# A recurrent stage that runs on centred values: mean sums left out, sums and activations moved

## The chip, the core and the metric

One core of a Trainium2 chip runs the whole program. The metric is device time in microseconds (us) of one execution. The engines named here are TensorE (PE, with its weight loads PEld), VectorE (DVE), ScalarE (ACT), GpSimd (POOL) and SyncE (SP, which issues DMAs).

## The reference

Two transformer blocks run one after the other on 512 tokens of width 1024. Of the second, one mixer matters here, an RWKV-7 recurrence with 16 heads of 64:

```python
def step(state, inp):
    r_t, w_t, k_t, v_t, aa_t, bb_t = inp
    sa = jnp.einsum('bhvk,bhk->bhv', state, aa_t)
    state = state * w_t[:, :, None, :] + sa[..., None] * bb_t[:, :, None, :] + v_t[..., None] * k_t[:, :, None, :]
    return state, jnp.einsum('bhvk,bhk->bhv', state, r_t)
...
mean = jnp.mean(y, axis=-1, keepdims=True)
var = jnp.mean(jnp.square(y - mean), axis=-1, keepdims=True)
y = ((y - mean) * lax.rsqrt(var + GN_EPS)).reshape(b, s, c) * lnx_w + lnx_b
bonus = (jnp.sum(r_h * k_h * r_k, axis=-1, keepdims=True) * v_h).reshape(b, s, c)
return ((y + bonus) * g).astype(z.dtype)
```

The mean is taken over the 64 value components of a head. `y` is linear in `v`, and each value component evolves by itself, so the `y` of values whose mean over the components was taken away is `y - mean`. The bonus uses the values as they are.

## The kernel before

Each engine has its own program, written out by hand, and semaphores order them. Weight products are split in three matmuls of 128x512 (high and low halves); one step `n` of `gate_part` is one of them, one step `n` of `rkv_slice` is three.

The recurrent stage goes over 8 pairs of heads (`PAIRS`); a pair fills the 128 partitions and has 8 chunks of 64 tokens. For pair q the stage has these parts, and pairs overlap:

- `wide_part(q)`. PE: `lora_products` (L1257, L1258), 24 steps of `rkv_slice` (L1229 to L1231; steps 0 to 7 make the key, 8 to 15 the receptance, 16 to 23 the value), and between them sums over the partitions of a head, matmuls with a block matrix of ones: `means` (L1279), `bonus_sums` (L1274), `variances` (L1284), `key_norms` (L1267), and the `gate` product (L1290, L1291). `means`, `variances` and `gate` are those of pair q-2, `bonus_sums` that of q-1. DVE: `centred` (L2497), `columns_of`, `log_decays` (L2449 to L2459), `take_key` (L2392, L2394, L2444), `take_bonus` (L2502), the receptance, `finished` (L2508 to L2515), the value. ACT: `sigmoids` (L1867, L1868), `squares_of_centred` (L1884), `decays`, `key_squares` (L1859), `deviations` (L1888), `key_lengths` (L1872).
- `decayed_keys(q)` on DVE (L2465 to L2484) makes the operands of the recurrence, and signals `rk.kr` after L2481.
- `gates(q)` on PE: 48 steps of `gate_part` (L1213), two outputs.
- `prepare(q, step)` on PE and `prepared(q)` on DVE: the 64x64 products of each chunk (L1347) and what takes them; the first, `gram(q, "D")`, waits for `rk.kr`. `turn` turns the values, `bT` and `kkT` by a product with the identity.
- `chain(p)`: the recurrence itself (L1444, L1483), with the steps of `prepare(p+1)` between its links. At its end ACT takes the result of bank 3 out (L1939).

After pair 7 the next stage starts when the last gates have been written to HBM, the residual has been read back (`x_kept`), and POOL has split the first weights of that stage.

POOL does nothing in this stage but split weight strips from `raws` into `whi` (L630) and `wlo` (L632), in two halves each. A strip is split once the products of the strip before it in the same buffer are done. Strip 0 of a pair holds the weights of steps 0 to 15 of `rkv_slice`; strip 2, the gates' weights, takes its place. So step 15 is what lets POOL begin on the gates' strip.

The stage opens with the merge of three attention groups: for four parts `pr`, ACT spreads factors (L1837), PE turns them (L1246), DVE multiplies and adds (L2408 to L2413). Then come ACT's tanh and sigmoids of the low-rank inputs (L1843 to L1845), `lora_products(0)`, 24 gate steps, `key_norms(0)`, 24 more gate steps, `wide_part(1)`, `prepare(0, ...)`.

## Time and profile before

| | |
|---|---|
| time, median of 3 runs | 2182.37 us (2175.4 to 2183.83) |
| time of the profiled execution | 2179.82 us |
| its span | 2178.1 us |
| PE busy / DVE busy / POOL busy / ACT busy | 2079.2 / 1221.7 / 1044.5 / 524.6 us |
| recurrent stage in the span | about 1104 to 1672 us |

In a timeline row the columns are start, duration (both us), engine, line, operation, output and inputs, shapes and count, and in brackets the idle time of the engine before it with what ended that. A time in the span is a position, not a duration.

### The profile page before, as it was taken

The page shows a single profiled execution, that of the slowest core. Times are in us where ns is not written, and L with a number is a line of the kernel's source. Part 1 is how long each engine was busy: PE and PEld are TensorE (multiplying, and loading weights), DVE is VectorE, ACT ScalarE, POOL GpSimd, SP SyncE. Part 2 cuts the span into 40 slices and gives each one's busy share as a digit, 9 for nine tenths or more (in the row PEclk, how much of TensorE's full clock was granted, in tenths as well). Part 3 has the DMA queues.
Part 4 walks back from the last instruction along what each step waited for, and adds up shares of the span by engine and source line. Part 5 has one row for each costly group of instructions (what it writes and reads, how often), then busy time and mean ns, then how long its engine had stood idle before and what let it go on. Part 6 is the DMA issues. An engine that isn't in the chain of part 4 may idle for free.

```text
span 2178.1 us, 39285 instructions
## 1 busy us (share of the span) xinstructions
PE 2079.2 (95%) x16109; PEld 1708.3 (78%) x16109; DVE 1221.7 (56%) x1577; ACT 524.6 (24%) x1132; POOL 1044.5 (48%) x764
## 2 busy tenths in 40 slices
PE   8999999899999989999988999999987999999998
PEld 6888787778777778788867888778875777888887
DVE  7888624466666662301176677776664546656423
ACT  2100002334343121312322212222313013333101
POOL 6777764335344355263453033332203665666663
PEclk9999999899999989999999999999998999999999
DMA  4333232244534331122322122211103332222221
GB/s 139 97 97 97 97 96 69 82 137 130 158 123 133 109 97 59 58 78 70 98 72 61 34 62 61 63 43 34 33 4 128 135 116 78 96 96 96 92 95 65
DMA packets 180341, 189.96 MB, mean 87 GB/s; under 512 B 8141, under 2 KB 161372, under 8 KB 179932
## 3 DMA queue, kind: packets, MB, share of 16 engines
q1 hardware_dynamic: 172288, 181.81, 26.4%
q10 hardware_dynamic: 7900, 5.94, 0.9%
q8 instruction: 116, 1.90, 0.4%
q14 instruction: 37, 0.30, 0.0%
HBM read 179.30 MB, written 8.44 MB: 86 GB/s over the span
## 4 chain that ended last, share of the span: by engine, by line
PE 54%; DVE 10%; DVEq 2%; DMA 2%; ACT 1%; issue 1%; ACTq 0%; POOL 0%; POOLq 0%; SPq 0%
PE bank L775 8%; PE bank L773 8%; PE bank L774 8%; PE bank L1347 6%; PE bank L1444 2%; PE bank L1213 1%; PE bank L1231 1%; PE bank L1229 1%; PE bank L1230 1%; DVE sq L2467 1%; PE bank L1177 1%; PE bank L1149 1%; PE bank L1151 1%; PE bank L1150 1%; PE bank L821 1%; DVE inv_E L2508 1%
## 5 line engine op out<-in xcount | busy, mean ns | idle before, releaser
L632 POOL TENSOR_TENSOR wlo<-raws,whi 128x1024 fp32r<-128x1024 f32 (+5 forms) x316 | 684.9, 2167 | 47.3 <-issue 5.2
L630 POOL TENSOR_SCALAR whi<-raws 128x1024 fp32r<-128x1024 f32 (+5 forms) x316 | 337.9, 1069 | 592.6 <-PE bank L1231 270.4
L773 PE MATMUL bank<-hbuf,whi 128*128 128x512 f32 (+2 forms) x840 | 328.5, 391 | 0.0
L775 PE MATMUL bank<-hbuf,wlo 128*128 128x512 f32 (+2 forms) x840 | 327.6, 390 | 0.0
L774 PE MATMUL bank<-hbuf,whi 128*128 128x512 f32 (+2 forms) x776 | 302.7, 390 | 0.0
L606 POOL TENSOR_TENSOR spare<-ones 1x1 f32<-1x1 f32 x100 | 25.3, 253 | 464.2 <-PE bank L775 252.9
L773 PEld LDWEIGHTS bank<-hbuf,whi 128*128 128x128 f32 (+2 forms) x840 | 157.2, 187 | 34.6 <-POOL wlo L632 1.1
L775 PEld LDWEIGHTS bank<-hbuf,wlo 128*128 128x128 f32 (+2 forms) x840 | 157.1, 187 | 34.4
L774 PEld LDWEIGHTS bank<-hbuf,whi 128*128 128x128 f32 (+2 forms) x776 | 145.1, 187 | 31.4
L2346 DVE TENSOR_REDUCE nmax<-bank 128x4 f32<-128x512 f32 (+3 forms) x40 | 21.1, 550 | 159.9 <-PE bank L1124 116.7
L1229 PE MATMUL bank<-hbuf,whi 128*128 128x512 f32 x192 | 87.9, 458 | 0.0
L1213 PE MATMUL bank<-hbuf,whi 128*128 128x512 f32 x256 | 84.3, 406 | 0.0
L1231 PE MATMUL bank<-hbuf,wlo 128*128 128x512 f32 x192 | 75.7, 394 | 0.0
L1230 PE MATMUL bank<-hbuf,whi 128*128 128x512 f32 x192 | 75.5, 393 | 0.0
L2198 DVE SCALAR_TENSOR_TENSOR adaacc<-adaw,vec,adaacc 128x768 f32<-128x768 f32 x56 | 71.6, 1278 | 5.4 <-DMA adaw<-in_w_ada 0.3
L773 PE MATMUL bank<-fH,whi 128*128 128x512 f32 x176 | 68.7, 390 | 0.0
L775 PE MATMUL bank<-fH,wlo 128*128 128x512 f32 x176 | 68.5, 389 | 0.0
L774 PE MATMUL bank<-fL,whi 128*128 128x512 f32 x176 | 68.5, 389 | 0.0
L908 PE MATMUL bank<-hbuf,whi 128*128 128x512 f32 x160 | 66.7, 417 | 1.1 <-DVE y2L L2183 0.9
L803 PE MATMUL bank<-hbuf,whi 128*128 128x512 f32 x128 | 54.3, 424 | 10.9 <-DVE hbuf L737 5.8
L910 PE MATMUL bank<-hbuf,wlo 128*128 128x512 f32 x160 | 62.8, 393 | 0.0
L652 ACT ACTIVATE sq<-xT 128x512 f32<-128x512 f32 x24 | 15.2, 632 | 185.6 <-DVE xT L2115 144.0
(482 smaller groups left out, 4676.3 us busy)
## 6 DMA issues: line engine op xcount, KB each, us to landing
adaw<-in_w_ada SPq DMA_DIRECT2D x64, 384.0 KB, 4.2
raws<-in_w_up SPq DMA_DIRECT2D x22, 1024.0 KB, 4.9
raws<-in_w_in SPq DMA_DIRECT2D x41, 512.0 KB, 4.3
raws<-in_w_in SPq DMA_DIRECT2D x18, 1024.0 KB, 4.9
raws<-in_pool_w_in SPq DMA_DIRECT2D x16, 1024.0 KB, 5.2
raws<-in_mla_w_in SPq DMA_DIRECT2D x10, 1024.0 KB, 5.9
raws<-in_pool_w_out SPq DMA_DIRECT2D x8, 1024.0 KB, 5.0
raws<-in_mla_w_out SPq DMA_DIRECT2D x8, 1024.0 KB, 5.4
```

Source lines behind the costliest of these rows:

```text
L630: G.tensor_scalar(h_, r_, 1.0, 1.0, ALU.mult, ALU.mult)
L632: G.tensor_tensor(l_, r_, f32(h_), ALU.subtract).then_inc(raw_split, 1)
L773: M.matmul(dst, wh, acts[k][0], start=(first and k == 0), stop=False)
L774: M.matmul(dst, wh, acts[k][1], start=False, stop=False)
L775: mm = M.matmul(dst, wl, acts[k][0], start=False, stop=(last and k == n - 1))
L908: M.matmul(dst, wh, act[0], start=first, stop=False)
L1213: mm = M.matmul(dst[:, :], wl if i == 2 else wh, h_out[k][int(i == 1)], start=(k == 0 and i == 0), stop=(k == DT - 1 and i == 2))
L1229: M.matmul(bank[z][:, :], wh, h_out[k][0], start=(k == 0), stop=False)
L1230: M.matmul(bank[z][:, :], wh, h_out[k][1], start=False, stop=False)
L1231: mm = M.matmul(bank[z][:, :], wl, h_out[k][0], start=False, stop=(k == DT - 1))
L1347: mm = M.matmul(dst[rows, cs], left[rows, cs], R, start=(start is None or c == start), stop=True, skip_group_check=True)
L2198: V.scalar_tensor_tensor(adaacc[:, :], adaw[n % 3][:, :], c_col, adaacc[:, :], ALU.mult, ALU.add)\
```

## The change

The values are turned by a product with `centre`, the identity less 1/64, instead of the identity. Everything of the recurrence that is linear in the values is then centred, and `means` (PE), `centred` (DVE) and the wait of `squares_of_centred` (ACT) go; ACT squares straight out of bank 3 at the end of the chain (`gn.q`). `variances` moves forward to just behind the first two steps of `rkv_slice` (in the last wide part, six gate steps). In `wide_part(1)` alone, `bonus_sums(0)` moves from behind step 7 to behind step 15, with a wait for the taken gates in its old place. `key_norms(0)` moves nine gate steps back. ACT's tanh and sigmoids move to behind the first and second spread of the merge. `centre` lies where an unused buffer of the same size was, and two small DVE instructions make it at the start.

```diff
@@ -233,7 +233,7 @@
-        margin = sb("margin", [P, 96])
+        centre = sb("centre", [P, 96])[:, 0:CH]
         raws = sb("raws", [P, 2 * 2048])
@@ -376,7 +376,7 @@
                              "E32": inv_E32, "N2": tile(hf, 0), "W": tile(hf, 0), "A2": tile(hf, 1), "Z": tile(hf, 1)}
-                    gn_y, gn_c, gn_sq, gn_dev = inv_DA, inv_U, inv_E16, inv_E32
+                    gn_x, gn_y, gn_sq, gn_dev = inv_DA, inv_U, inv_E16, inv_E32
         with ExitStack() as st:
@@ -1263,7 +1263,7 @@
                 elif q >= 2:
-                    pe.wait_ge(sem("gn.y"), q - 1)
+                    pe.wait_ge(sem("gn.q"), q - 1)
                 M.matmul(bank[3][:, :], same[64][:, :], tile(sq, 0), start=True, stop=True)\
@@ -1273,11 +1273,6 @@
                     .then_inc(sem("rk.bs"), 1)
-
-            def means(p):
-                pe.wait_ge(sem("gn.y"), p + 1)
-                M.matmul(bank[4][:, :], same[64][:, :], gn_y[:, :], start=True, stop=True)\
-                    .then_inc(sem("gn.m"), 1)
@@ -1298,16 +1293,18 @@
                 lora_products(q)
+                rkv(0, 2)
                 if q >= 2:
-                    means(q - 2)
-                rkv(0, 8)
+                    variances(q - 2)
+                rkv(2, 8)
                 if q >= 2:
                     pe.wait_ge(sem("inv.dve"), q * TAKEN_ALL)
-                bonus_sums(q - 1)
-                rkv(8, 12)
-                if q >= 2:
-                    variances(q - 2)
-                rkv(12, 16)
+                    bonus_sums(q - 1)
+                else:
+                    pe.wait_ge(sem("gt.taken"), 2)
+                rkv(8, 16)
+                if q == 1:
+                    bonus_sums(0)
                 key_norms(q)
@@ -1328,22 +1325,25 @@
-                means(PAIRS - 2)
-                for n in range(9):
+                for n in range(6):
+                    gate_part(PAIRS - 1, n)
+                variances(PAIRS - 2)
+                for n in range(6, 9):
                     gate_part(PAIRS - 1, n)
...
                 bonus_sums(PAIRS - 1)
-                variances(PAIRS - 2)
                 for n in range(9, 3 * DT):
...
+            identity = chunk_mask["id"]
+
             def chunk_products(dst, left, right, lo=0, hi=CHUNKS, start=None):
...
                     for rows in HEAD_ROWS:
-                        R = ident[rows, rows] if right is None else right[rows, cs]
+                        R = right[rows, 0:CH] if right is identity or right is centre else right[rows, cs]
                         mm = M.matmul(dst[rows, cs], left[rows, cs], R, start=(start is None or c == start),
@@ -1365,8 +1365,8 @@
-            def turn(b, x, signal):
-                chunk_products(bank[b], x, None).then_inc(sem(signal), 1)
+            def turn(b, x, signal, by=identity):
+                chunk_products(bank[b], x, by).then_inc(sem(signal), 1)
@@ -1381,7 +1381,8 @@
                     pe.wait_ge(sem("inv.dve"), q * TAKEN_ALL + levels_taken(k))
-                chunk_products(bank[LEVEL_BANK[k][w]], inv_t[left], None if right == "I" else inv_t[right])                    .then_inc(sem(f"inv.pe{w}"), 1)
+                chunk_products(bank[LEVEL_BANK[k][w]], inv_t[left],
+                               identity if right == "I" else inv_t[right]).then_inc(sem(f"inv.pe{w}"), 1)
@@ -1397,7 +1398,7 @@
                     pe.wait_ge(sem("rk.ge"), q * 8 + GRAM_TAKEN["ak"])
-                    turn(7, vT[q % 2], "rk.tv")
+                    turn(7, vT[q % 2], "rk.tv", centre)
                 elif step == 7:
@@ -1492,9 +1493,11 @@
                 gate_part(0, n)
+            pe.wait_ge(evac[0], fill("rkv", 0) + 1)
+            for n in range(3 * DT, 3 * DT + 9):
+                gate_part(0, n)
             key_norms(0)
-            pe.wait_ge(evac[0], fill("rkv", 0) + 1)
-            for n in range(3 * DT, 6 * DT):
+            for n in range(3 * DT + 9, 6 * DT):
                 gate_part(0, n)
@@ -1508,7 +1511,6 @@
                     last_wide_part()
-            means(PAIRS - 1)
             variances(PAIRS - 1)
@@ -1836,13 +1838,15 @@
                            f.unsqueeze(3).to_broadcast([P, 4, 2, 64])).then_inc(sem("cmb.f"), 1)
-
-
-            for b in (0, 2, 3):
-                act.wait_ge(evac[b], fill("lora", b) + 1)
-            A.activation(wlow[0:64, :], wlow[0:64, :], ACT.Tanh).then_inc(sem("lora.act"), 1)
-            A.activation(tile(glow, 0), tile(glow, 0), ACT.Sigmoid)
-            A.activation(glow[0:32, S:2 * S], glow[0:32, S:2 * S], ACT.Sigmoid).then_inc(sem("lora.act"), 1)
+                if pr == 0:
+                    act.wait_ge(evac[0], fill("lora", 0) + 1)
+                    A.activation(wlow[0:64, :], wlow[0:64, :], ACT.Tanh).then_inc(sem("lora.act"), 1)
+                if pr == 1:
+                    for b in (2, 3):
+                        act.wait_ge(evac[b], fill("lora", b) + 1)
+                    A.activation(tile(glow, 0), tile(glow, 0), ACT.Sigmoid)
+                    A.activation(glow[0:32, S:2 * S], glow[0:32, S:2 * S], ACT.Sigmoid).then_inc(sem("lora.act"), 1)
+
@@ -1879,10 +1883,6 @@
-            def squares_of_centred(p):
-                act.wait_ge(sem("gn.c"), p + 1)
-                A.activation(gn_sq[:, :], gn_c[:, :], ACT.Square).then_inc(sem("gn.q"), 1)
-
             def deviations(p):
@@ -1896,8 +1896,6 @@
                         load_lora(q + 1)
-                if q >= 2:
-                    squares_of_centred(q - 2)
                 if more:
@@ -1933,10 +1931,9 @@
                 act.wait_ge(sem("sq.y"), p + 1)
-                if p + 1 < PAIRS:
-                    act.wait_ge(sem("inv.pe0"), (p + 1) * MADE_ALL[0] + level_made(0, 4))
                 act.wait_ge(sem("rk.y"), p + 1)
                 A.activation(gn_y[:, :], bank[3][:, :], ACT.Copy, scale=SCAN_SCALE ** -2).then_inc(sem("gn.y"), 1)
+                A.activation(gn_sq[:, :], bank[3][:, :], ACT.Square, scale=SCAN_SCALE ** -2).then_inc(sem("gn.q"), 1)
@@ -1954,7 +1951,6 @@
             load_gate(PAIRS - 1)
-            squares_of_centred(PAIRS - 1)
             deviations(PAIRS - 1)
@@ -2050,6 +2046,7 @@
                     V.tensor_copy(chunk_mask[name][r, :], x[r, r])
+                V.tensor_scalar(centre[r, :], ident[r, r], 1.0 / CH, None, ALU.subtract)
             V.tensor_reduce(res4[:, :], ident[:, :].rearrange("p (k r) -> p r k", r=4), AX.X, ALU.add)
@@ -2492,22 +2489,17 @@
-            def centred(p):
-                dve.wait_ge(sem("gn.m"), p + 1)
-                V.scalar_tensor_tensor(gn_c[:, :], bank[4][:, :], -1.0 / 64, gn_y[:, :], ALU.mult, ALU.add)\
-                    .then_inc(sem("gn.c"), 1)
-
             def take_bonus(q):
...
-                x, pc = gn_y, pcol[p % 3]
+                x, pc = gn_x, pcol[p % 3]
                 dve.wait_ge(sem("gn.s"), p + 1)
...
                 dve.drain()
-                V.scalar_tensor_tensor(x[:, :], gn_c[:, :], pc[:, 8:9], gn_dev[:, :], ALU.mult, ALU.mult)
+                V.scalar_tensor_tensor(x[:, :], gn_y[:, :], pc[:, 8:9], gn_dev[:, :], ALU.mult, ALU.mult)
                 dve.drain()
@@ -2518,7 +2510,7 @@
                 if q >= 2:
-                    centred(q - 2)
+                    dve.wait_ge(sem("gn.y"), q - 1)
                 if more:
@@ -2606,7 +2598,6 @@
             take_last_gates()
-            centred(PAIRS - 1)
             finished(PAIRS - 1)
...
```

## Rows read from the trace of the kernel before

**Rows 1.** Page, part 1: busy time, share of the span, instructions.
```profile
PE 2079.2 (95%) x16109; PEld 1708.3 (78%) x16109; DVE 1221.7 (56%) x1577; ACT 524.6 (24%) x1132; POOL 1044.5 (48%) x764
```
**Rows 2.** Windows: stretch, its length, busy of each engine, granted clock, DMA.
```profile
1157.00:1162.00 5.00, 5.00 (x11) 3.19 (x11) 1.99 (x6) 3.83 (x4) 0.00 (x0) 0.50 0.05 13
1240.00:1305.00 65.00, 63.48 (x1074) 52.95 (x1072) 45.56 (x59) 16.80 (x39) 18.99 (x12) 1.00 0.18 53
```
**Rows 3.** Timeline of wide part 2 and the chain after it.
```profile
1237.02 0.60 ACT L1939 ACTIVATE inv_DA<-bank 128x512 f32<-128x512 f32 x1 [0.43 <-PE bank L1444]
...
1239.15 1.12 PE L1279 MATMUL bank<-inv_DA,same 128*128 128x512 f32 x2
...
1240.31 0.69 DVE L2497 SCALAR_TENSOR_TENSOR inv_U<-bank,inv_DA 128x512 f32<-128x512 f32 x1 [1.42 <-PE bank L1279]
...
1253.03 0.75 DVE L2392 TENSOR_SCALAR Rr<-bank,pcol 128x512 f32<-128x512 f32 x1 [2.63 <-PE bank L1231]
1253.16 1.05 POOL L630 TENSOR_SCALAR whi<-raws 128x1024 fp32r<-128x1024 f32 x1 [40.05 <-PE bank L1231]
...
1275.83 1.15 PE L1347 MATMUL bank<-aT,bT 64*64 64x64 f32 x32 [0.53 <-DVE rT L2481]
```
**Rows 4.** Chain that ended last, wide part 4: start, length, what.
```profile
1368.37 1.05 PE bank L1279 x2
...
1378.53 0.86 PE bank L1284 x2
```
**Rows 5.** Timeline of ACT in the merge, and at the first decays.
```profile
1110.53 1.14 ACT L1837 COPY ap<-fac 128x512 f32<-128x512 f32 x2 [1.62 <-PE bank L1246]
...
1115.96 1.14 ACT L1837 COPY ap<-fac 128x512 f32<-128x512 f32 x2 [3.77 <-PE bank L1246]
...
1123.60 1.28 ACT L1844 ACT_TABLE_LOAD   x1
...
1145.75 0.63 ACT L1876 ACTIVATE epos<-cc 128x512 f32<-128x512 f32 x1 [1.77 <-DVE lwd L2459]
```
**Rows 6.** Timeline from the first gates to the end of wide part 1.
```profile
1139.66 1.13 PE L1267 MATMUL bank<-sq,same 128*128 128x512 f32 x2 [1.42 <-ACT sq L1859]
...
1156.70 2.08 PE L1274 MATMUL bank<-Rr,same 128*128 128x512 f32 x2 [3.70 <-DVE Rr L2484]
...
1159.96 0.43 DVE L2449 TENSOR_SCALAR lwd<-lwd 128x512 f32<-128x512 f32 x1 [2.69 <-ACT inv L1868]
1160.46 1.23 DVE L2451 TENSOR_TENSOR_SCAN cc<-restart,lwd 128x512 f32<-128x512 f32 x1
...
1162.86 0.69 DVE L2459 TENSOR_TENSOR lwd<-cc,lwd 128x512 f32<-128x512 f32 x1
...
1166.01 1.04 POOL L630 TENSOR_SCALAR whi<-raws 128x1024 fp32r<-128x1024 f32 x1 [15.51 <-PE bank L1231]
1166.34 1.13 PE L1267 MATMUL bank<-sq,same 128*128 128x512 f32 x2 [0.49 <-ACT sq L1859]
...
1172.98 0.75 DVE L2392 TENSOR_SCALAR vT<-bank,pcol 128x512 f32<-128x512 f32 x1 [5.28 <-PE bank L1231]
```
**Rows 7.** Timeline: DVE instructions issued while POOL runs one.
```profile
1129.04 2.35 POOL L632 TENSOR_TENSOR wlo<-raws,whi 128x1024 fp32r<-128x1024 f32 x1
1129.86 2.07 DVE L2411 TENSOR_TENSOR num<-num 128x512 f32<-128x512 f32 x1
...
1262.83 2.41 POOL L632 TENSOR_TENSOR wlo<-raws,whi 128x1024 fp32r<-128x1024 f32 x1
...
1264.19 1.33 DVE L2465 TENSOR_SCALAR sq<-sq 128x512 f32<-128x512 f32 x1
```
**Rows 8.** One line of DVE: count, duration ns min/median/max, first and last start.
```profile
L2510 DVE SCALAR_TENSOR_TENSOR inv_DA<-inv_U,pcol,inv_E x8: 752/2695/2695, 1258.1 to 1663.4; 128x512 f32<-128x512 f32 x8
```
**Rows 9.** Chain that ended last, from the last chain to the next stage.
```profile
1655.99 2.67 DMA gates_kept<-xT
1659.05 9.45 DMA raws<-in_w_att_out
...
1671.60 0.79 PE bank L821
```

## The prediction, made before the result was known

> **What bounds the kernel now.** I read the page first: PE is busy nearly all of the span, and nothing else comes near [rows 1]. Then the chain that ended last, over the recurrent stage. It alternates: PE through the first two thirds of a wide part, then DVE, then PE and DVE link by link. A timeline of one wide part shows the seams [rows 3]. DVE waits 2.63 us for the receptance product (step 15) at 1253.03. From there it works without a pause to `rk.kr`, and PE, which has meanwhile done the gates, waits only 0.53 us for it at 1275.83. So a wide part is set by PE up to step 15, and then by DVE with PE just behind: what PE saves before step 15 moves both, and is gained in full. The clock is 1.00 there [rows 2].
>
> The opening is another matter [rows 6]. PE waits 3.70 us for the first bonus operand at 1156.70, then computes steps 8 to 15 at a granted clock of 0.50, which is 1.2 GHz [rows 2], and is through just before `key_norms(1)`, which waits 0.49 us for the squares. Those come from DVE's list: decays from 1159.96, then the key. Steps 16 to 23 follow at full clock and end with DVE's take of the value at 1172.98, DVE having waited 5.28. So there the order is DVE up to the squares, then PE.
>
> **Means and centring in the wide parts.** `means` is two matmul instructions that take 1.05 on the chain, its sister `variances` 0.86 [rows 4]. The extra 0.19 stands behind `lora_products`, and I take it that whatever comes next pays it. Saving 0.86 for each of seven: wide parts 2 to 7 and the last. That is 6.0 us; at most 7 x 1.05 = 7.4. `variances` is moved, not added. It waits for ACT's new square: the copy ends at 1237.62, a square of the same form takes 0.60 too, so `gn.q` comes at about 1238.2, and PE is at `means` only at 1239.15 [rows 3] and at the new place later still. Behind that wait stand the key steps, untouched. DVE loses its 1.42 wait and the 0.69 of the centring [rows 3], and its decays start some 2 us sooner, but it waits 2.63 at step 15 afterwards, so nothing comes of it beyond PE's 0.86. If that wait were not there, DVE would set the pace and `means` be worth nothing. ACT's square is in its list either way.
>
> **The last pair.** After it PE waits for a chain of DMAs: the last gates are written, then `x_kept` and the weights are read, 9.45 us, and PE begins at 1671.60 [rows 9]. That chain starts at the last gate product, which the change leaves where it is. The norm of pair 7 is ready sooner (1.05 of `means`, 0.69 of centring, some 0.3 between: 2 us), and that is hidden: 0, at most 2.0.
>
> **Tanh and sigmoids in the merge.** ACT has 1.62 us free before the second spread and 3.77 before the third [rows 5]. An activation of this size takes 0.60 [rows 3]: the tanh fits the first gap, a table load of 1.28 and two sigmoids (1.2) fit the second. They do not hold up the spreads, and PE did not wait for them where they were (it waited for DVE's last multiplication). 0 both ways. Without the slack it would cost 0.6 + 1.28 + 1.2 = 3.1.
>
> **`key_norms(0)` nine steps later.** PE waited 1.42 for it [rows 6], and now waits about that longer for the receptance instead, then does nine steps and the norm. It reaches `wide_part(1)` 0.86 later. ACT's lengths and decays come up to 2.6 later against 1.77 of slack [rows 5], and DVE has the whole norming of the keys before it asks for them: 0. PE's 0.86 disappears in the 3.70 wait.
>
> **`bonus_sums(0)` behind step 15.** PE no longer stands still in front of the bonus operand. It had steps 0 to 7 done at 1156.70 - 3.70 = 1153.0; with the 0.86 that is 1153.9. Eight steps at full clock last what they last behind `key_norms(1)`: 1172.98 - 1166.34 less 1.05 for the norm's matmuls, 5.6. So step 15 is done at 1159.5, where it was done just before 1166.01. That gains nothing by itself, for `key_norms(1)` still waits for DVE's and ACT's squares. It does two other things.
>
> First, it lets POOL loose. POOL had waited 15.51 us for step 15 and began at 1166.01 [rows 6]. Now it begins at 1159.6, and its four instructions (1.05, 2.4, 1.05, 2.4) lie on top of DVE's decays. The trace shows what that does [rows 7]: L2411, issued at 1129.86 under a POOL instruction that ends at 1131.39, ends at 1131.93, 0.54 behind it, and takes 2.07; L2465 takes 1.33 and ends 0.28 behind POOL's. DVE instructions on SBUF operands stand until POOL's is over, and get one turn between two of POOL's. Worked through: L2449 ends at 1160.9 (POOL's first is over at 1160.65); POOL's second until 1163.3; the scan L2451 then, until 1164.4; POOL's third until 1165.45, and the small copy; POOL's fourth until 1168.0; L2455 until 1168.5; the rest to 1169.4. The decays ended at 1163.55 [rows 6], so they are 5.9 late. No row shows a scan under a POOL instruction; if it runs through, the same sum gives 1168.4, 4.9 late. I take 5.4. If nothing collided it would be 0.5 or less, from small shifts of the split before it.
>
> The Trainium skill, "SBUF — State Buffer", section "Who interferes with whom", says that GpSimd and VectorE share one pair of ports as an exclusive lock, and that a VectorE instruction with two SBUF inputs is blocked as well. The rows agree for L2411; by that rule the scan is blocked, and the sum below would be 0.5 higher.
>
> Second, PE now idles from about 1160.4 until the squares at about 1171.7, three times as long as in the 3.70 after which it worked at half clock [rows 2, 6]. So the norm and steps 16 to 23 are slow instead of steps 8 to 15, and nothing hides them: a sum and eight steps lasted 1166.01 - 1156.70 = 9.3 after the idle, against 1172.98 - 1166.34 = 6.6 warm. That is 2.7 more; 0 if the clock stays.
>
> **Small things.** Two 64x64 instructions on DVE at the start, each at most the 0.43 of a 128x512 one [rows 6]: 0.2. The turning product has the same shape, 0.
>
> **The sum.** -6.0 + 5.4 + 2.7 + 0.2 = +2.3 on the profiled execution's 2179.8, so 2182.1. The median of the runs is 2.5 above that execution, and the forecast against it is 2182.4 + 2.3 = 2184.7. What a measurement of this kernel can tell from no change is about 0.5%, 10.9 us, so this is no measurable change.
>
> **Rivals.**
> - *The forecast, opening loses what the wide parts gain:* 2184.7, between -7.4 + 4.9 + 2.9 = +0.4 (2182.8) and -6.0 + 5.9 + 2.9 = +2.8 (2185.2), and 3 more to each side for the measurement. Chance 0.47.
> - *POOL does not hurt.* DVE wins the turns or POOL comes too late; the cold clock stays. -6.0 + 0.5 + 2.7 + 0.2 = -2.6, 2179.8. For it: which engine goes first decides, and the rows have only one order. Against it: six DVE instructions on SBUF in a row. Chance 0.20.
> - *The opening costs nothing, and all of `means` and the last pair counts:* -7.4 - 2.0 = -9.4, 2173.0. For it: half clock and lock both depend on small shifts. Against it: 9.45 us of DMA in front of the next stage. Chance 0.17.
> - *The change does not do what it says:* DVE is the bound in the wide parts after all, and the 0.86 is not gained. +8.3, 2190.7. For it: PE's wait at 1275.83 is for DVE. Against it: DVE's own wait of 2.63. Chance 0.08.
> - *Slower.* In the wide parts too the phase of DVE and POOL shifts. L2510 stands behind POOL in most pairs now (2.695 against 0.752) [rows 8]; were one more instruction caught, it costs 1.94 in each of six parts, 11.7: 2184.7 + 11.7 = 2196.4. It decides from 8.6 us more than the forecast, 1.4 a part. Against it: DVE and POOL are both released by step 15, within 0.13 of each other [rows 3], and stay so. Chance 0.08.
>
> **How the numbers follow.** The likeliest case gives 2184.7. A range from 2174 to 2192 leaves out the slower case and half of the fast one, 0.16 to 0.2, and takes in both ends of the collision and of the clock. Faster by over 0.5% needs more than 10.9 us, which no case gives alone; a third of the fast case with luck in the measurement: 0.06. Slower: the last case and some of the one before it, 0.09. The rest, 0.85, is within 0.5%.
>
> **What would show it.** Means: no L1279; from one wide part to the next 0.86 less than now, (1368.37 - 1239.15) / 2 = 64.6 [rows 3, 4]. Opening: POOL L630 released at about 1159.6 instead of 1166.0, L2455 or L2451 two to three times as long as now, `key_norms(1)` with an idle of some 11 us before it, a granted clock of 0.50 behind it, and the value taken at about 1181 instead of 1172.98. End: PE's wait for POOL at the next stage longer by about 2, its start as far behind the last gate product as now. The prediction is wrong if `gn.q` holds PE at `variances`, if the key steps are not what DVE waits for, or if POOL's earlier start brings a transfer forward that delays another.

## The result, and the profile after

The changed kernel took 2185.75 us in the median of 20 runs, and the kernel before 2182.11 in the median of 20 runs on the same chip: +3.6 us. Three of these 40 runs were slow, 2611.53 to 3455.23 us, and are left out of the ratio. It is 1.0021, with a 95% interval from 1.0014 to 1.0028, so 3.1 to 6.1 us. The forecast was 2184.7, +2.3. By the 0.5% that the chances were drawn with, this is no change. The interval excludes 1, so with so many runs a small loss is measurable, and it also excludes the +2.3: the loss is larger than the sum said.

The profiled execution took 2186.43, with a span of 2184.7. Part 1 of its page, which answers to [rows 1]:

```profile
PE 2070.0 (95%) x16093; PEld 1703.5 (78%) x16093; DVE 1217.3 (56%) x1571; ACT 524.2 (24%) x1132; POOL 1045.0 (48%) x764
```

PE has 16 matmul instructions fewer and is 9.2 us less busy, and the span is longer. So PE stands idle somewhere. Three stretches tell where.

**The wide parts.** The timeline of wide part 2 in the kernel after (L1279 is now `variances`, L2389 the take of a product, L2478 the last key step):

```profile
1219.31 1.10 PE L1347 MATMUL bank<-aT,bT 64*64 64x64 f32 x32
...
1248.83 1.02 PE L1279 MATMUL bank<-inv_E,same 128*128 128x512 f32 x2
...
1260.35 0.75 DVE L2389 TENSOR_SCALAR Rr<-bank,pcol 128x512 f32<-128x512 f32 x1 [3.57 <-PE bank L1231]
...
1283.15 1.15 PE L1347 MATMUL bank<-aT,bT 64*64 64x64 f32 x32 [0.54 <-DVE rT L2478]
...
1536.82 1.15 PE L1347 MATMUL bank<-aT,bT 64*64 64x64 f32 x32 [0.53 <-DVE rT L2478]
```

The first and the last of the same products (L1347, the first Gram product of a pair) in the kernel before:

```profile
1211.68 1.10 PE L1347 MATMUL bank<-aT,bT 64*64 64x64 f32 x32
...
1533.39 1.15 PE L1347 MATMUL bank<-aT,bT 64*64 64x64 f32 x32 [0.53 <-DVE rT L2481]
```

There is one norm product where [rows 3] had `means` at 1239.15 and `variances` later, and nothing holds it. DVE's wait for the receptance product grew from 2.63 to 3.57: it is idle longer, so PE still sets the pace there. PE's wait for the key steps is what it was (0.54 against 0.53). From one Gram product to the next the five periods from 1219.31 to 1536.82 are 63.50 in the mean. Before, from 1211.68 to 1533.39, they were 64.34. That is 0.84 less in each. The sixth period, up to the last pair, is 61.09 where it was 61.97.

**The opening.** The timeline from the first key steps to the take of the value, in the kernel after (L2446 to L2456 are the decays):

```profile
1148.02 0.62 POOL L630 TENSOR_SCALAR whi<-raws 128x512 fp32r<-128x512 f32 x1 [12.83 <-PE bank L1213]
...
1148.86 1.76 DVE L2466 TENSOR_TENSOR kk<-kk,sq 128x512 f32<-128x512 f32 x1
1150.70 0.93 DVE L2469 SCALAR_TENSOR_TENSOR aT<-kk,lwd 128x512 f32<-128x512 f32 x1
1151.56 1.77 DVE L2470 TENSOR_TENSOR bT<-kk,inv 128x512 f32<-128x512 f32 x1
...
1160.20 1.04 POOL L630 TENSOR_SCALAR whi<-raws 128x1024 fp32r<-128x1024 f32 x1 [7.41 <-PE bank L1231]
1160.87 0.65 DVE L2446 TENSOR_SCALAR lwd<-lwd 128x512 f32<-128x512 f32 x1 [2.69 <-ACT inv L1872]
1161.39 2.34 POOL L632 TENSOR_TENSOR wlo<-raws,whi 128x1024 fp32r<-128x1024 f32 x1
1161.59 3.21 DVE L2448 TENSOR_TENSOR_SCAN cc<-restart,lwd 128x512 f32<-128x512 f32 x1
1163.69 1.95 POOL L630 TENSOR_SCALAR whi<-raws 128x1024 fp32r<-128x1024 f32 x1
1164.88 0.79 DVE L2450 COPY mid<-cc 128x8 f32<-128x8 f32 x1
...
1165.79 2.84 POOL L632 TENSOR_TENSOR wlo<-raws,whi 128x1024 fp32r<-128x1024 f32 x1
1166.51 2.14 DVE L2455 TENSOR_TENSOR fade<-cc,mid 128x7 f32<-128x7 f32 x1
1168.58 0.68 DVE L2456 TENSOR_TENSOR lwd<-cc,lwd 128x512 f32<-128x512 f32 x1
...
1172.05 2.08 PE L1267 MATMUL bank<-sq,same 128*128 128x512 f32 x2 [11.16 <-ACT sq L1863]
...
1180.20 0.75 DVE L2389 TENSOR_SCALAR vT<-bank,pcol 128x512 f32<-128x512 f32 x1 [6.78 <-PE bank L1231]
```

And the window behind PE's idle time (columns as in [rows 2]; the last two figures are DMA):

```profile
1172.00:1176.00 4.00, 3.95 (x9) 2.50 (x10) 1.34 (x2) 1.88 (x2) 0.00 (x0) 0.60 0.00 0
```

POOL begins at 1160.20 where it began at 1166.01 [rows 6], and DVE's decays interleave with it. The scan takes 3.21 instead of 1.23. The copy of eight elements a row takes 0.79 and the product of seven 2.14, as each waits for a turn. PE does nothing for 11.16 us, and its next product takes 2.08, as one did after the idle of 3.70 [rows 6]. The granted clock behind it is 0.60 in the mean of four us, so a part of them ran at 1.2 GHz; from 1176 on it is 1.00. The value is taken at 1180.20 instead of 1172.98. `lora_products(0)` came 0.84 earlier (1129.03, before at 1129.87). The merge itself is as long as before, the whole stage began 0.81 earlier in this execution. So from `lora_products(0)` to the take of the value the opening costs 7.22 + 0.84 = 8.1. Three parts make it up. The decays begin 1.75 later after `lora_products(0)` (31.84 against 30.09), before POOL touches them. They take 4.80 longer. From `key_norms(1)` to the take there are 8.15 where there were 6.64, 1.51 more.

**The last pair.** Timeline from the last gates to the next stage, kernel after:

```profile
1657.86 0.37 SPq L507 DMA_DIRECT2D gates_kept<-xT  x1
...
1668.60 4.90 DVE L2608 TENSOR_TENSOR rL<-yr,rH 128x512 fp32r<-128x512 f32 x8
1670.26 3.29 POOL L606 TENSOR_TENSOR spare<-ones 1x1 f32<-1x1 f32 x1 [85.66 <-DMA raws<-in_w_att_out]
...
1675.60 0.80 PE L821 MATMUL bank<-atH,whi 128*128 128x512 f32 x1 [14.60 <-POOL wlo L632]
```

From the write of the gates to PE's start there are 17.74 us, where there were 15.61 (1655.99 to 1671.60, [rows 9]). POOL's instruction on a single element, the first that it does when the weights have landed, took 3.29, where it took 0.61 before.

Between `lora_products(0)` and PE's start on the next stage there are 546.57 us, before 541.73: 4.8 more. The spans of the two profiled executions differ by 6.6. The rest lies outside of the stage (0.84 earlier ahead of it, 2.6 later behind it), where the change does next to nothing.

### The profile page after: what moved, and what is told of

Same layout as the page of the kernel before. It is cut to its first block, busy times and chain, and to the rows that moved or that the text cites. A ratio compares the mean times of both kernels' runs of the same rounds, so it can differ in the third digit from the quotient of the medians.

```text
span 2184.7 us, 39249 instructions
## 1 busy us (share of the span) xinstructions
PE 2070.0 (95%) x16093; PEld 1703.5 (78%) x16093; DVE 1217.3 (56%) x1571; ACT 524.2 (24%) x1132; POOL 1045.0 (48%) x764
## 4 chain that ended last, share of the span: by engine, by line
PE 53%; DVE 9%; DMA 2%; DVEq 2%; issue 1%; ACT 1%; POOL 1%; POOLq 0%; ACTq 0%; SPq 0%
PE bank L775 8%; PE bank L774 8%; PE bank L773 8%; PE bank L1347 7%; PE bank L1445 2%; PE bank L1213 1%; PE bank L1229 1%; PE bank L1231 1%; PE bank L1230 1%; DVE sq L2464 1%; PE bank L1177 1%; PE bank L1149 1%; PE bank L1151 1%; PE bank L1150 1%; DVE inv_E L2500 1%
## 5 line engine op out<-in xcount | busy, mean ns | idle before, releaser
L1213 PEld LDWEIGHTS bank<-hbuf,whi 128*128 128x128 f32 x256 | 48.2, 189 | 17.1 <-DVE Rr L2391 4.2
```

The costliest lines, as they stand in the source:

```text
L1213: mm = M.matmul(dst[:, :], wl if i == 2 else wh, h_out[k][int(i == 1)], start=(k == 0 and i == 0), stop=(k == DT - 1 and i == 2))
```

## The experiments

The time beside each is the median of its own runs. The kernel before ran on the same chip with each group of them: 2181.74 (bonus product back, POOL held, POOL held with PE at work, bonus product alone), 2181.31 (both back, with the wait, the wait in the changed kernel) and 2181.35 (the other four). A difference from before is from that of its own group, and two kernels of different groups are compared by these differences; the changed kernel's is +3.6. None of these differences is good to a tenth. The 95% intervals reach 2 to 3 us to each side, and more where two experiments are set against each other. In the text cold stands for a granted clock of 0.50 (1.2 GHz), warm for 1.00 (2.4 GHz).

### `bonus_sums(0)` back in its old place

```
-                    bonus_sums(q - 1)
-                else:
-                    pe.wait_ge(sem("gt.taken"), 2)
-                rkv(8, 16)
-                if q == 1:
-                    bonus_sums(0)
+                bonus_sums(q - 1)
+                rkv(8, 16)
```

> The changed kernel, with bonus_sums(0) back behind step 7 of wide part 1. Theory: its place behind step 15 cost 8.1 us (POOL's split on top of DVE's decays 5.4, half clock behind the long idle 2.7), so this runs 8.1 under the changed kernel, 4.5 under the kernel before (-0.2%). Rival (the opening costs nothing, the loss sits at the end of the stage or is luck): like the changed kernel, 3.6 above the kernel before.

2181.21, 0.5 under the kernel before; ratio 0.9997 (0.9988 to 1.0006). Against the changed kernel that is 3.6 + 0.5 = 4.1 gained. It should have been 4.5 under before, so 4 are missing: something else costs too. In its timeline the second norm product is this:

```profile
1168.75 2.01 PE L1267 MATMUL bank<-sq,same 128*128 128x512 f32 x2 [2.21 <-ACT sq L1859]
```

PE waited 2.21 for the squares, where it had waited 0.49 [rows 6], and it worked at half clock behind so short an idle (granted 1.00 from 1166.50 to 1168.70, 0.53 from there to 1171.00).

### POOL held back, clock left cold

The changed kernel, with POOL made to wait before the first split of the gates' strip until DVE has the key of pair 1:

```
+                        if ph == "rkv" and i == 1 and j == 2:
+                            pool.wait_ge(sem("rk.kk"), 2)
```

> The changed kernel, in which POOL waits with the gates' strip of pair 1 until DVE has made the key of pair 1. Nothing else moves. Theory: the port collision is 5.4 to 5.9 of the loss, so 1.8 to 2.3 under the kernel before; the scan takes 1.23 again instead of 3.21, key_norms(1) idles some 6 us instead of 11.16 and is still followed by half clock (2.08 for its two matmuls). Rival (the clock or the order alone costs it): 3.6 above the kernel before, key_norms(1) as late as in the changed kernel.

2180.43, 1.3 under before; ratio 0.9998 (0.9989 to 1.0007). Against the changed kernel 3.6 + 1.3 = 4.9 gained. Its timeline:

```profile
1141.97 1.02 PE L1269 MATMUL bank<-sq,same 128*128 128x512 f32 x2
...
1160.11 1.23 DVE L2450 TENSOR_TENSOR_SCAN cc<-restart,lwd 128x512 f32<-128x512 f32 x1
...
1165.45 1.04 POOL L632 TENSOR_SCALAR whi<-raws 128x1024 fp32r<-128x1024 f32 x1 [14.53 <-DVE kk L2443]
...
1165.98 2.08 PE L1269 MATMUL bank<-sq,same 128*128 128x512 f32 x2 [6.51 <-ACT sq L1865]
...
1175.51 0.75 DVE L2391 TENSOR_SCALAR vT<-bank,pcol 128x512 f32<-128x512 f32 x1 [8.17 <-PE bank L1233]
```

The scan is back at 1.23, and the norm comes 6.3 us sooner after `lora_products(0)` than in the changed kernel (36.75 against 43.02). Not all of that is POOL's doing: in this execution the clock stayed at full through `key_norms(0)` (1141.97), and the decays already began 1.5 sooner. The other 4.8 are the decays, 3.58 long against 8.39. The cold clock behind `key_norms(1)` stays.

### POOL held back, and PE kept at work

The same, and 24 products without use behind `bonus_sums(0)`:

```
+                    for n in range(24):
+                        M.matmul(bank[4][:, :], h_out[1][0][:, 0:P], h_out[0][0], start=True, stop=True)
```

> As the one before, and PE fills its idle time ahead of key_norms(1) with 24 matmuls of 128x512 into a bank that nobody reads (5.4 us of work, not part of the computation). Theory: the clock stays at full, another 2.7 is gained: 4.5 under the kernel before; the value is taken 6.6 behind the start of key_norms(1) instead of 8.15. Rival (the clock costs nothing): like the one before, or up to 1 us slower.

2177.87, 3.9 under before; ratio 0.9983 (0.9974 to 0.9992). It is 2.6 under the run without these products. Its timeline, with POOL's first instruction for the next stage:

```profile
1165.94 1.13 PE L1269 MATMUL bank<-sq,same 128*128 128x512 f32 x2 [0.88 <-ACT sq L1867]
...
1172.59 0.75 DVE L2393 TENSOR_SCALAR vT<-bank,pcol 128x512 f32<-128x512 f32 x1 [5.28 <-PE bank L1233]
...
1663.62 0.31 POOL L606 TENSOR_TENSOR spare<-ones 1x1 f32<-1x1 f32 x1 [86.45 <-DMA raws<-in_w_att_out]
```

The norm takes 1.13 instead of 2.08, and from its start to the take of the value there are 6.65 instead of 9.53: 2.9 for the clock, where POOL is held back. The 2.6 between the medians is not that price alone. The norm stands 1.5 later after `lora_products(0)` than in the run above, whose first norm ran at full clock. And in this execution POOL's instruction on one element took 0.31 and PE started the next stage 15.19 behind the write of the gates, 17.73 in the run above.

### `bonus_sums(0)` moved, alone, in the kernel before

```
-                bonus_sums(q - 1)
+                    bonus_sums(q - 1)
+                else:
+                    pe.wait_ge(sem("gt.taken"), 2)
...
+                if q == 1:
+                    bonus_sums(0)
```

> The kernel before, with the move of bonus_sums(0) behind step 15 alone. Theory: it costs 8.1 by itself: 2190 where the kernel before takes 2182 (+0.37%). Rival (the loss comes from the parts together): no change.

2189.84, 8.1 above before; ratio 1.0035 (1.0021 to 1.0048), so between 4.6 and 10.5. Its timeline shows both signs with nothing else changed:

```profile
1161.69 3.22 DVE L2455 TENSOR_TENSOR_SCAN cc<-restart,lwd 128x512 f32<-128x512 f32 x1
...
1172.15 2.07 PE L1267 MATMUL bank<-sq,same 128*128 128x512 f32 x2 [11.16 <-ACT sq L1863]
```

One thing differs from the kernel before that the edit doesn't touch. The first norm, `key_norms(0)`, took 2.07 in this execution and 1.13 in the profiled one of before, and the decays began 1.68 later after `lora_products(0)`. So the 8.1 holds a cold first half of the opening too.

### Both products of the opening back

The first edit, and `key_norms(0)` in its old place:

```
+            key_norms(0)
             pe.wait_ge(evac[0], fill("rkv", 0) + 1)
-            for n in range(3 * DT, 3 * DT + 9):
-                gate_part(0, n)
-            key_norms(0)
-            for n in range(3 * DT + 9, 6 * DT):
+            for n in range(3 * DT, 6 * DT):
```

> The changed kernel with bonus_sums(0) and key_norms(0) both back in their old places: centring and the moved activations alone. Theory: seven times 0.86, 6.0 under the kernel before, less what DVE's earlier end costs at the start of the next stage (2.1 in the profiled execution of the changed kernel): 4 to 6 under. Against the kernel with only bonus_sums(0) back, key_norms(0) accounts for 0 to 1. Rival (the wide parts gain nothing): no change.

2177.84, 3.5 under before, where 4 to 6 were expected; ratio 0.9982 (0.997 to 0.9994). It ran again in a later group:

> bonus_sums(0) and key_norms(0) both back, the same program as the earlier one with both back: how well 3.5 us under the kernel before repeats beside the others of this call. 3 to 6 under.

2177.33, 4.0 under; ratio 0.9976 (0.9966 to 0.9986). With the bonus product alone put back it was 0.5 under, so the kernel with `key_norms(0)` nine steps later is 3.0 to 3.5 slower, which the prediction had at 0. What is left are the centring, the earlier `variances` and the merge, and the six us expected of them are not all there: the end is still as in the changed kernel. The timeline of the first of the two runs:

```profile
1660.11 4.90 DVE L2602 TENSOR_TENSOR rL<-yr,rH 128x512 fp32r<-128x512 f32 x8
1661.79 3.26 POOL L606 TENSOR_TENSOR spare<-ones 1x1 f32<-1x1 f32 x1 [85.71 <-DMA raws<-in_w_att_out]
...
1667.10 0.79 PE L821 MATMUL bank<-atH,whi 128*128 128x512 f32 x1 [14.61 <-POOL wlo L632]
```

### The end: DVE waits for POOL's first strip

Before the fifth low half of the next stage, DVE waits until POOL has split the first half strip of that stage's weights:

```
                 dve.wait_ge(sem("mx.hi"), k + 1)
+                if k == 4:
+                    dve.wait_ge(raw_split, split_value(STRIP0["mix"], 0))
```

On top of both products back:

> As the one before, and DVE waits with the low halves of the recurrence's output until POOL has split the first half strip of the next stage. Theory: POOL's one-element instruction no longer stands 3.29 us behind DVE: 2.1 less than the one before, 6 to 8 under the kernel before. Rival (the DMA sets the start anyway, or DVE's later splits hold PE later): no change against the one before.

2175.95, 5.4 under before, where 6 to 8 were expected; ratio 0.9971 (0.9961 to 0.9981). In its timeline POOL's one-element instruction is short again:

```profile
1665.89 0.18 POOL L606 TENSOR_TENSOR spare<-ones 1x1 f32<-1x1 f32 x1 [85.83 <-DMA raws<-in_w_att_out]
```

Once more, in the later group:

> Both back, and DVE waits with the low halves until POOL's first half strip is split, again: 2 under the one without that wait if the port lock at the end is real; the rival says equal.

2176.02, 5.3 under; ratio 0.9966 (0.9954 to 0.9978). The wait gained 1.9 in the one group and 1.3 in the other; each by itself is within the noise. In the traces, from the write of the gates to PE's start on the next stage there are 14.70 us in both of these runs, where the two of "both back" have 17.74 and 17.73. And in the changed kernel as it is:

> The changed kernel with that wait of DVE alone. Theory: 2.1 less than the changed kernel, 1.5 above the kernel before. Rival: like the changed kernel, 3.6 above.

2182.74, 1.4 above before; ratio 1.0005 (0.9995 to 1.0015), where the changed kernel is 3.6 above: 2.2 gained. In its trace the stretch is 16.02, against 17.74.

### `key_norms(0)` moved, alone, in the kernel before

The edit of "both back", the other way round.

> The kernel before, with the move of key_norms(0) behind nine gate steps alone. The kernel with only bonus_sums(0) put back ran 0.5 us under the kernel before where 4.5 was expected, and the one with both put back 3.5 under; the difference is laid to this move: a longer first idle of PE brings half clock, POOL's split of the value strip comes 2.3 later and falls on DVE's key work. Theory now: 2 to 4 us above the kernel before. Rival (the first prediction: the 0.86 disappears in a wait): no change.

2184.74, 3.4 above before by the medians; ratio 1.0008 (0.9999 to 1.0017), so between nothing and 3.7. By itself this does not show a loss. The timeline of this run:

```profile
1140.47 1.22 PE L1213 MATMUL bank<-hbuf,whi 128*128 128x512 f32 x2 [3.75 <-DVE Rr L2396]
...
1149.66 0.62 POOL L630 TENSOR_SCALAR whi<-raws 128x512 fp32r<-128x512 f32 x1 [13.58 <-PE bank L1213]
...
1150.67 1.60 DVE L2471 TENSOR_TENSOR kk<-kk,sq 128x512 f32<-128x512 f32 x1
1152.35 0.93 DVE L2474 SCALAR_TENSOR_TENSOR aT<-kk,lwd 128x512 f32<-128x512 f32 x1
1153.21 1.78 DVE L2475 TENSOR_TENSOR bT<-kk,inv 128x512 f32<-128x512 f32 x1
```

and the kernel before at the same place, rows that the prediction did not look at:

```profile
1146.13 3.35 DVE L2467 RECIPROCAL sq<-sq 128x512 f32<-128x512 f32 x1
1146.42 0.62 POOL L630 TENSOR_SCALAR whi<-raws 128x512 fp32r<-128x512 f32 x1 [10.38 <-PE bank L1213]
...
1149.56 1.49 DVE L2469 TENSOR_TENSOR kk<-kk,sq 128x512 f32<-128x512 f32 x1
1151.13 0.69 DVE L2472 SCALAR_TENSOR_TENSOR aT<-kk,lwd 128x512 f32<-128x512 f32 x1
1151.74 0.68 DVE L2473 TENSOR_TENSOR bT<-kk,inv 128x512 f32<-128x512 f32 x1
```

Before, POOL's split of the value strip lies under DVE's reciprocal and is nearly over when the key steps begin. In this execution the last gate product is done later, POOL starts 3.24 later, and three key steps take 4.31 instead of 2.86. The same is to be seen in the changed kernel (1.76, 0.93, 1.77).

But with the clock at full the move makes only 0.8 of these 3.2. The trace with POOL held back has the move, and its clock stayed at full: there `lora_products(1)` starts 17.13 behind `lora_products(0)`, against 16.31 before. Here it is 19.52. The granted clock was 0.50 from 1140.40 to 1144.00; in the kernel before it was 1.00 from 1138.00 to 1146.20. And a cold first half does the same with the norm in its old place. Positions after `lora_products(0)`, from the timelines:

| execution | `key_norms(0)` in its place, its duration | `lora_products(1)` | decays | `key_norms(1)` | take of the value |
|---|---|---|---|---|---|
| before | old, 1.13 | 16.31 | 30.09 | 36.47 | 43.11 |
| both back, first and later | old, 1.13 and 1.13 | 16.30, 16.32 | 30.07, 30.09 | 36.45, 36.46 | 43.09, 43.08 |
| both back and the wait at the end, first and later | old, 2.08 and 2.07 | 19.05, 19.14 | 31.63, 31.72 | 38.78, 38.83 | 47.02, 47.08 |
| bonus product moved alone | old, 2.07 | 19.19 | 31.77 | 43.46 | 51.58 |
| key norm moved alone | moved, 1.60 | 19.52 | 32.61 | 39.77 | 47.96 |
| bonus product back | moved, 1.85 | 18.72 | 31.81 | 38.98 | 47.27 |
| POOL held | moved, 1.02 | 17.13 | 30.38 | 36.75 | 46.28 |
| POOL held, PE at work | moved, 1.57 | 18.75 | 31.85 | 38.22 | 44.87 |
| changed kernel | moved, 1.91 | 18.75 | 31.84 | 43.02 | 51.17 |

Up to the take of the value, the third row and "bonus product back" differ by the place of the norm alone, and end within 0.3 of each other; the second and third row have the same opening, instruction by instruction, and end 4.0 apart. So it is the cold first half that costs some 4 us, and the move costs, beside its 0.8, only what it adds to the chance of that. Of these executions three of six are cold with the norm in its old place, and five of six with the norm moved (the changed kernel with the wait at the end, not in the table, is the sixth: 18.75). That is too few to show that the move brings the cold clock.

### The opening kept warm

The best version so far, with 12 products without use before `lora_products(0)` and 6 before `key_norms(0)`:

```
+            pe.wait_ge(sem("att.num"), 12)
+            for n in range(12):
+                M.matmul(bank[7][:, :], h_out[1][0][:, 0:P], h_out[0][0], start=True, stop=True)
...
+            for n in range(6):
+                M.matmul(bank[4][:, :], h_out[1][0][:, 0:P], h_out[0][0], start=True, stop=True)
             key_norms(0)
```

> As the one before, and PE fills two idle times of the opening with work that is not part of the computation: 12 matmuls of 128x512 ahead of lora_products(0), 6 ahead of key_norms(0). Theory: in some executions of one and the same program the clock falls to half after the first idle and the opening is 2.7 to 4 us longer, so holding the clock takes 1 to 3 us off the median: 7 to 9 under the kernel before. Rival (DVE sets the opening, the clock there costs nothing): no change against the one before.

2176.4, 5.0 under before, where 7 to 9 were expected; ratio 0.9963 (0.9949 to 0.9977). With so few runs it can't be told from the version without (2176.02). The clock did stay at 1.00 through the first half, as the window shows (columns as in [rows 2]), and `lora_products(1)` came 16.38 behind `lora_products(0)`. But the value was taken at 46.44, where the warm openings of the table have 43.1:

```profile
1128.00:1145.00 17.00, 15.23 (x64) 10.96 (x64) 15.16 (x25) 5.94 (x9) 6.47 (x4) 1.00 0.26 74
```

The timeline of the same run:

```profile
1154.96 1.12 PE L1274 MATMUL bank<-Rr,same 128*128 128x512 f32 x2 [3.71 <-DVE Rr L2480]
...
1161.71 1.05 POOL L630 TENSOR_SCALAR whi<-raws 128x1024 fp32r<-128x1024 f32 x1 [12.94 <-PE bank L1231]
...
1163.40 2.12 DVE L2440 TENSOR_SCALAR kk<-Kr,pcol 128x512 f32<-128x512 f32 x1
...
1166.24 1.58 PE L1267 MATMUL bank<-sq,same 128*128 128x512 f32 x2 [4.70 <-ACT sq L1862]
```

PE did steps 8 to 15 at full clock too, so POOL was let loose sooner (33.64 behind `lora_products(0)`, 36.17 in the first run of "both back"). It fell on the key of pair 1 (2.12; 0.49 where nothing is in its way, as in the run with POOL held back). PE waited 4.70 for the squares and was slow again. It is the mechanism of the moved bonus product once more, set off by a faster PE. This reading is from one trace, and no further run tested it.

## Why the prediction was right, point by point

**The sum.** Forecast +2.3, measured +3.6 (3.1 to 6.1). The likeliest case is the one that came, and its two main mechanisms are there. The number is partly luck: two terms that the sum had at 0 cost about 2 each in the trace, and two others were too large by 0.6 and 1.2. Its terms, one by one:

| term | predicted | measured |
|---|---|---|
| means gone, seven wide parts | -6.0 | 0.84 a period in the trace, x 7 = -5.9 |
| POOL's splits on the decays | +5.4 | 4.80 in the trace after |
| half clock behind `key_norms(1)` | +2.7 | 1.51 in the trace after; 2.9 where POOL is held |
| both, bonus product moved alone | +8.1 | +8.1 by medians, 4.6 to 10.5, with a cold first half in its trace |
| key norm nine steps later | 0 | +1.75 at the decays in the trace after, +0.3 in the one with a warm first half |
| last pair | 0, at most 2.0 gained | 2.1 lost in the trace; the wait that undoes it gained 1.3, 1.9 and 2.2 by medians |

**Means.** Right in place and size. DVE's wait at step 15 grew and PE's at the Gram product stayed. The rival in which DVE is the bound is out.

**Bonus product.** Counted from `lora_products(0)`, POOL was released at 31.17, forecast 29.7 (1159.6 less 1129.87); the value was taken at 51.17, forecast some 51.1; the idle was 11.16, forecast some 11. That the take falls on the forecast is luck: 1.75 + 4.80 + 1.51 = 8.06 were forecast as 0 + 5.4 + 2.7. Between start and end of the decays, from 1160.87 to 1169.26, there are 8.39 us, and before 3.59 [rows 6]: 4.8 more, just under the 4.9 to 5.9. The scan was blocked, though, and the higher end was meant for that: the decays started 0.67 behind POOL's release where the sum had 0.36, and the product of seven ended 0.02 behind POOL's fourth instruction where the sum had 0.5. The clock cost 1.5 and not 2.7 in the changed kernel, as it was back at 1.00 four us after the norm's start; in the run with POOL held it was still 0.50 until 1172.00, six us after it, and cost 2.9.

The Trainium skill, "SBUF — State Buffer", section "Who interferes with whom", states that a VectorE instruction with two SBUF inputs contends with a GpSimd instruction that reads SBUF. For the scan, of which the rows before had no case, the trace after agrees: 3.21 against 1.23.

**The key norm.** This step was wrong as it stood: "PE's 0.86 disappears in the 3.70 wait". PE's 0.86 is there (0.82 in the trace with a warm first half), but the step had the clock at full and nothing queued behind it. In five of six traces with the move PE goes on at half clock behind its first idle, so the last gate product of pair 0 comes up to 3.2 later. It releases POOL's split of the value strip, which had lain under DVE's reciprocal and now lies on the key steps, and the decays begin 1.7 to 2.5 later. The same happens in three traces with the norm in its old place, so the runs do not show that the move is the cause. This is also why the gains do not add up. The bonus move costs 3.9 when the first half is cold anyway (51.17 against 47.27 for "bonus product back"; 4.1 by the medians). It costs 8.1 to 8.5 counted from a warm opening. Undoing both from the changed kernel gains 3.6 + 3.5 = 7.1 or 3.6 + 4.0 = 7.6. The expectation for the kernel with the bonus product put back was 4 too low for the same reason: its opening was cold, 47.27 where the warm one has 43.1.

**The last pair.** The wrong sign. The step took the chain of transfers as the whole path and a sooner norm as hidden. Before, POOL's one-element instruction came first (1668.69, 0.61 long) and DVE's eight low halves (from 1669.17) took turns with POOL's splits, 14.26 us in all. Now the norm of pair 7 is ready sooner, the low halves run back to back from 1668.60, 4.90 in all, and POOL stands behind them for 3.29. The wait that reverses this order removes it (0.18), in two kernels, and brings PE's start forward by 3.0 in the one and 1.7 in the other. So the sooner norm costs here, through the order of the two engines, but not in every execution: in the run with POOL held and PE at work the low halves came first too, by 1.01, and POOL got in after 0.31. Why it did there is open.

**The slower rival.** L2510, now L2502, has a median of 2.53 us over its eight instances, 2.70 before [rows 8], and the wide parts got shorter. No further DVE instruction was caught there: over the five periods each of DVE's other lines has the mean duration it had, within 0.02.

**Merge.** ACT's waits before the second and third spread are 1.08 and 1.30 now, 1.62 and 3.77 before [rows 5]. Tanh and sigmoids fit, as worked out: from the first spread to `lora_products(0)` there are 22.59, before 22.62.

**What is left.** -5.9 + 8.1 + 2.1 = 4.3 by these terms, 4.8 by the stage as a whole in the trace, and 3.6 by the medians. Runs of one program range over 8 to 10 us, and a warm or a cold first half alone makes 4.0, so the rest can't be settled.

The best version is the centring with both products of the opening in their old places and DVE's wait at the end: 2176.0, 5.3 us under the kernel before (0.997), and so 8.9 under the changed one. Of the change, centring is the part that pays. The two moves in the opening together cost more than it gives (7.1 to 7.6 against some 6). The earlier `variances` and the merge had no run of their own.

## What to carry to other kernels

Moving a product on a busy engine also moves what its end releases. Before calling a move free, look up who waits for each product on the way, and what the engine that it lets loose will run against: here POOL's splits and DVE's work on the same memory, three times over. And before laying a few us to an edit, look whether the two profiled executions ran the stretches ahead of it at the same clock: here one and the same opening took 43.1 or 47.0. Work that comes sooner than it is needed can cost as much as work that comes late, when it takes the turn of the instruction on which the end hangs; one wait that puts these two in order can be worth more than one of the products saved.

## What the runs showed of the hardware that was not expected

**A one-element instruction can wait 3.29 us.** DVE's low halves take 4.90 / 8 = 0.61 each, and POOL's instruction got in only when all were over (3.29, 3.26 in the first run of "both back", 2.06 in the later one, where the weights landed later), while elsewhere the two took turns (1.04, 0.65, then 2.34, 3.21 in the decays). Where nothing was in its way it took 0.18. With the same code at the end it took 0.31 in the run with POOL held and PE at work, so this too differs between executions.

**The clock falls after short idles, and not in every execution.** The first norm product stands behind an idle of 3 us in both runs of one opening, here in the timeline of the later run of "both back":

```profile
1139.50 1.13 PE L1267 MATMUL bank<-sq,same 128*128 128x512 f32 x2 [3.01 <-ACT sq L1857]
```

And the timeline of the same opening with the wait at the end, in the same group:

```profile
1139.34 2.07 PE L1267 MATMUL bank<-sq,same 128*128 128x512 f32 x2 [3.00 <-ACT sq L1857]
```

The one ran on at 2.4 GHz, the other at 1.2. From `lora_products(0)` to `lora_products(1)` there were 16.3 us in the first and 19.1 in the second. An idle of 2.21 was enough in the first experiment, and one of 3.71 was not in the last. It costs more than the slow products: the one opening ended 43.08 behind `lora_products(0)`, the other 47.08. What decides between the two is open.
